# Two-layer decoder trunk: the up projections computed with x loaded and W moving, and transposed back through DVE squares and SBUF transfers

## The reference

```python
def causal_dwconv(x, w, b):      # width 3 here: each channel's own three taps over the sequence, plus a bias
    ...
def conv_ffn(h, w_up, conv_w, conv_b, w_down):
    u = causal_dwconv(h @ w_up, conv_w, conv_b)
    gate, val = jnp.split(u, 2, axis=-1)
    return (jax.nn.gelu(gate) * val) @ w_down

# in the trunk, for each layer:
#   x = x + mixer(rmsnorm(x, norm_mix));  x = x + conv_ffn(rmsnorm(x, norm_ffn), ...)
```

## The kernel before, in words

| stage | ACT | DVE |
|---|---|---|
| 2 | copy of the cross term (L387), after the block's last chunk | sum of the halves into h (L1006), then h times 1/rms (L1008) |
| 3 | last tap and bias into buf, 4 instructions (L430) | |
| 4, 5 | | the other two taps, 4 instructions each (L1102, L1108) |
| 6 | gelu, gate block (L434) | product of the halves, value block (L1118) |
| 7 | rounding into act (L438) | the rest into act (L1123), value block |

## Time and profile before

### The profile page before, as it was taken

One profiled execution on the slowest core, in us unless ns is written; L12 is line 12 of the kernel. 1 busy time (PEld: TensorE's weight loads), 2 busy tenths in 40 slices (PEclk: granted clock), 3 DMA queues, 4 the chain that ended last, 5 costly groups with the idle time before them and its releaser, 6 DMA issues.

```text
span 2245.3 us, 33233 instructions
## 1 busy us (share of the span) xinstructions
PE 2237.8 (100%) x12182; PEld 1930.9 (86%) x12182; DVE 1488.7 (66%) x1789; ACT 1158.0 (52%) x1452; POOL 7.7 (0%) x17
## 2 busy tenths in 40 slices
PE   9999999999999999999999999999999999999999
PEld 8888888888888888888888888888888888888887
DVE  7886766777677767545565556566777777674443
ACT  6654355555555555443455555555555555553333
POOL 0000000000000000000000000000000000000000
PEclk9999999999999999999999999999999999999999
DMA  7555655666666666556665454555656666666664
GB/s 271 185 175 165 193 173 187 185 190 188 187 188 191 190 186 189 189 185 196 194 219 177 158 189 161 167 185 172 196 178 195 182 191 187 187 190 212 203 202 140
DMA packets 216099, 420.93 MB, mean 187 GB/s; under 512 B 13029, under 2 KB 13045, under 8 KB 215888
## 3 DMA queue, kind: packets, MB, share of 16 engines
q1 hardware_dynamic: 214128, 413.59, 59.1%
q0 software_dynamic: 1456, 5.65, 0.7%
q10 hardware_dynamic: 432, 0.56, 0.1%
HBM read 417.62 MB, written 2.12 MB: 187 GB/s over the span
## 4 chain that ended last, share of the span: by engine, by line
PE 99%; DMA 0%; DVE 0%; ACT 0%; ACTq 0%; issue 0%
PE ps L685 48%; PE ps L689 24%; PE ps L738 5%; PE ps L739 5%; PE ps L740 5%; PE ps L711 4%; PE ps L713 4%; PE ps L712 4%; PE ps L777 0%; DMA x_res<-x_t 0%; PE ps L821 0%; PE ps L832 0%; PE ps L759 0%; PE ps L778 0%; PE ps L840 0%; PE ps L771 0%
## 5 line engine op out<-in xcount | busy, mean ns | idle before, releaser
L990 DVE TENSOR_TENSOR w_lo<-raw,w_hi 128x1024 fp32r<-128x1024 f32 x783 | 948.6, 1223 | 558.5 <-ACT w_hi L376 539.9
L376 ACT ACTIVATE w_hi<-raw 128x1024 fp32r<-128x1024 f32 x783 | 811.1, 1054 | 567.0 <-PE ps L689 358.1
L685 PE MATMUL ps<-xs,w_hi 128*128 128x512 f32 x3456 | 1086.7, 396 | 3.3 <-DVE w_lo L1419 2.7
L689 PEld LDWEIGHTS ps<-xs,w_lo 128*128 128x128 f32 x3456 | 649.2, 188 | 153.4
L689 PE MATMUL ps<-xs,w_lo 128*128 128x256 f32 x3456 | 679.1, 278 | 0.0
L685 PEld LDWEIGHTS ps<-xs,w_hi 128*128 128x128 f32 x3456 | 526.2, 189 | 4.5 <-DVE xs L1039 2.9
L685 PE MATMUL ps<-act,w_hi 128*128 128x512 f32 (+1 forms) x1216 | 382.3, 396 | 0.0
L689 PEld LDWEIGHTS ps<-act,w_lo 128*128 128x128 f32 x1216 | 228.4, 188 | 54.0
L689 PE MATMUL ps<-act,w_lo 128*128 128x256 f32 (+1 forms) x1216 | 239.0, 278 | 0.0
L685 PEld LDWEIGHTS ps<-act,w_hi 128*128 128x128 f32 x1216 | 185.2, 189 | 0.1
L738 PE MATMUL ps<-w_hi,xs 128*128 128x512 f32 x448 | 176.0, 393 | 0.0
(11 more groups left out here) (191 smaller groups left out, 1125.5 us busy)
## 6 DMA issues: line engine op xcount, KB each, us to landing
raw<-w_up SPq DMA_DIRECT2D x352, 512.0 KB, 3.7
raw<-w_in SPq DMA_DIRECT2D x191, 512.0 KB, 4.0
raw<-w_down SPq DMA_DIRECT2D x176, 512.0 KB, 4.7
raw<-w_out SPq DMA_DIRECT2D x64, 512.0 KB, 4.7
bias<-bias_line POOLq DMA_DIRECT2D x1, 2048.0 KB, 11.6
x_res<-x_t SPq DMA_DIRECT2D x3, 512.0 KB, 7.2
out_t<-x_res POOLq DMA_DIRECT2D x3, 512.0 KB, 5.8
gates_w<-w_gates POOLq DMA_DIRECT2D x1, 1024.0 KB, 5.3
```

Source lines behind the costliest of these rows:

```text
L376: act_f(w_hi[:, s, :, :], raw[:, s, :, :], ACT.Copy).then_inc(hi_ready, 1)
L685: return mm(ps[:, 4 * group + m, :], w_hi[:, s, u, m * P:(m + 1) * P], rhs, start=first and u == 0, stop=False)
L689: return mm(ps[:, 4 * group + m, 0:S], w_lo[:, s, u, m * P:(m + 1) * P], rhs[:, 0:S], start=False, stop=last and u == CT - 1)
L990: tt(w_lo[:, s, :, :], raw[:, s, :, :], w_hi[:, s, :, :].bitcast(F32), ALU.subtract).then_inc(lo_ready, 1)
```

## The change

The up projections of both layers take `chunk_values` in place of `chunk_products`. Their result comes out with the sequence on partitions, in two banks (4*half and 4*half + 1). The convolution needs channels on partitions, so it is turned in two steps:

1. DVE transposes the 32 x 32 squares of the two banks into `flip` (the place of `cross`): two instructions of 128 x 512. The ACT copy of the cross term and the DVE sum into h are gone.
2. SP issues sixteen transfers of 32 partitions x 1 KB, in four groups `move(n, i)`, i = 0 to 3, that bring each band of squares to its partitions in h. Group 0 is issued after the load of chunk 6 of the next block and waits for the transposes, group 1 after the load of chunk 7, groups 2 and 3 after the loads of chunks 0 and 1 of the block after that.

The sequence lies in h in another order, four segments of 64; the order of xs for the up projections is changed to fit (`x_seq`, `xs_seq`), for which DVE's `split_x` takes eight instructions of 128 columns instead of four of 256. The convolution's buffers have two more columns, zeroed once a layer, so that taps can be written shifted.

The stages move: the scaling by 1/rms to stage 7 (it waits for all sixteen transfers), the ACT tap to 8, the DVE taps to 9 and 10, gelu and product to 11, the rounding to 12 and the rest to 13. Stage 8 + c of a block runs in chunk c of the second block after it, ahead of stage c of the block before. The down projection's first block has its 22 chunks written out, with the last stages and moves among them.

```diff
-        self.cross_down = self.cross_up + 2 * PAIRS
+        self.cross_down = self.cross_up
...
+    flip = cross[:, :, :].rearrange("p b s -> p (b s)")
+    flip_by_seq = flip.rearrange("p (g k t r) -> p t g k r", g=QUADS, t=2, r=SQ)
+    flip_from = ps[:, :, :].rearrange("p b (k g c) -> p b g k c", g=QUADS, c=SQ)
+    flip_quads = flip.rearrange("p (g n) -> p g n", g=QUADS)
+    h_quads = h[:, :, :].rearrange("p b s -> p (b s)").rearrange("p (i n) -> p i n", i=QUADS)
+    h_tiles = h_quads.rearrange("p i (k n) -> p i k n", k=BT)
...
+        def move(n, i):
+
+            if i == 0:
+                sp.wait_ge(acc_drained, n + 1)
+            for g in range(QUADS):
+                sp.dma_start(h_quads[g * SQ:(g + 1) * SQ, i, :], flip_quads[i * SQ:(i + 1) * SQ, g, :]).then_inc(moved, 16)
...
-            with sp.Fori(0, PAIRS) as j:
+            for half in range(2):
+                for c in range(KC):
+                    load(w_up[l], ph.q_up + 2 * half, c, slice(half * D_FF, half * D_FF + NB), c)
+                    if half and c >= 6:
+                        move(ph.n_up, c - 6)
+            with sp.Fori(1, PAIRS) as j:
                 for half in range(2):
                     for c in range(KC):
                         load(w_up[l], ph.q_up + 4 * j + 2 * half, c, bass.ds(j * NB + half * D_FF, NB), c)
+                        if c < 2:
+                            move(ph.n_up + 2 * j + half - 2, 2 + c)
+                        if c >= 6:
+                            move(ph.n_up + 2 * j + half - 1, c - 6)
...
                 for c in range(KC):
                     split(ph.q_up + 4 * j, c)
+                    mlp_post(KC + c, ph, 0, j - 1)
                     mlp_post(c, ph, 1, j - 1)
                 for c in range(KC):
                     split(ph.q_up + 4 * j + 2, c)
+                    mlp_post(KC + c, ph, 1, j - 1)
                     mlp_post(c, ph, 0, j)
...
-                        chunk_products(ph.q_up + 4 * j + 2 * half, c, xs, CT * c, half, c == 0, c == KC - 1)
+                        chunk_values(ph.q_up + 4 * j + 2 * half, c, 4 * half, c == 0, c == KC - 1)
...
-            if stage == 2:
-                copy_cross(n, chunk_end(ph.q_up + 4 * j + 2 * half, KC - 1), half)
-            if stage == 3:
+            if stage == 8:
                 eng.wait_ge(normed, ph.normed_up + 2 * j + half + 1)
                 for t in range(BT):
...
-                    ins = act_f(buf[:, t, :], h[:, t, :], ACT.Identity, scale=w, bias=b)
+                    ins = act_f(by_quad(pad[:, t, 0:S]), h_tiles[:, :, t, :], ACT.Identity, scale=w, bias=b)
...
             if stage == 2:
-                drain_normed(n, ph.cross_up + 2 * j + half + 1, ph.normed_up + 2 * j + half + 1, half, h[:, :, :])
-            if stage == 4:
+
+                eng.wait_ge(chunk_used, chunk_end(ph.q_up + 4 * j + 2 * half, KC - 1))
+                step(v.transpose(flip_by_seq[:, 0], flip_from[:, 4 * half]))
+                v.transpose(flip_by_seq[:, 1], flip_from[:, 4 * half + 1]).then_inc(acc_drained, 1)
+                eng.wait_ge(acc_drained, n + 1)
+            if stage == 7:
+                eng.wait_ge(moved, 16 * QUADS * QUADS * (k + 1))
+                r = by_quad(rstd[:, 0:S])
+                scale = bass.AP(r.tensor, r.offset, [r.ap[0], r.ap[1], [0, BT], r.ap[2]])
+                tt(h_tiles, h_tiles, scale, ALU.mult).then_inc(normed, 1)
+                eng.wait_ge(normed, ph.normed_up + 2 * j + half + 1)
+            if stage == 9:
 
                 eng.wait_ge(tap_first, k + 1)
...
-                    ins = stt(out=buf[:, t, 2:S], in0=h[:, t, 0:S - 2], scalar=conv_at(ph.layer, 0, half, j, t),
-                              in1=buf[:, t, 2:S], op0=ALU.mult, op1=ALU.add)
+                    to = by_quad(pad[:, t, 2:S + 2])
+                    ins = stt(out=to, in0=h_tiles[:, :, t, :], scalar=conv_at(ph.layer, 0, half, j, t),
+                              in1=to, op0=ALU.mult, op1=ALU.add)
```

More of the change, by code:

```diff
@@ L38 @@
 PAIRS = D_FF // NB
+SQ = 32
+QUADS = P // SQ
 OUTB = D // NB
@@ L225, in build @@
     dve_step, act_step = sem("dve_step"), sem("act_step")
+    moved = sem("moved")
     tap_first, conv_done, gelu_done = sem("tap_first"), sem("conv_done"), sem("gelu_done")
@@ L310, in _ @@
                         load(w_up[l], ph.q_up + 4 * j + 2 * half, c, bass.ds(j * NB + half * D_FF, NB), c)
+                        if c < 2:
+                            move(ph.n_up + 2 * j + half - 2, 2 + c)
+                        if c >= 6:
+                            move(ph.n_up + 2 * j + half - 1, c - 6)
             for b in range(OUTB):
                 cols = slice(b * NB, (b + 1) * NB)
-                for c in DOWN_HEAD:
+                for c in range(FC) if b == 0 else DOWN_HEAD:
                     load(w_down[l], ph.q_down, FC * b + c, cols, c)
+                    if b == 0 and c in (0, 1, 8, 9):
+                        move(ph.n_down - 2 + c // 8, 2 + c % 8)
+                    if b == 0 and c in (6, 7):
+                        move(ph.n_down - 1, c - 6)
+                if b == 0:
+                    continue
                 with sp.Fori(*DOWN_TURNS) as t:
@@ L391, in split_x @@
             for t in range(j * BT, (j + 1) * BT):
-                ins = act_f(xs[:, t, 0, :], x_res[:, t, :], ACT.Copy, scale=param("gain", norm * KT + t))
+                to, x = xs[:, t, 0, :], x_res[:, t, :]
+                if norm % 2:
+                    to, x = xs_seq(to), x_seq(x)
+                ins = act_f(to, x, ACT.Copy, scale=param("gain", norm * KT + t))
             ins.then_inc(xs_hi, 1)
@@ L429, in mlp_post @@
                     b = conv_b_at(ph.layer, half, j, t)
[L430 removed]
+                    ins = act_f(by_quad(pad[:, t, 0:S]), h_tiles[:, :, t, :], ACT.Identity, scale=w, bias=b)
                 ins.then_inc(tap_first, 1)
[L432 removed]
+            if stage == 11 and half == 0:
                 eng.wait_ge(conv_done, k + 1)
[L434 to L435 removed]
+                act_f(pad_g[:, :, 0:S], pad_g[:, :, 0:S], ACT.Gelu_apprx_tanh).then_inc(gelu_done, 1)
+            if stage == 12 and half == 1:
                 g = ph.layer * PAIRS + j
                 eng.wait_ge(prod_ready, g + 1)
[L438 removed]
+                act_f(act[:, bass.ds(j * BT, BT), 0, :], pad_v[:, :, 0:S], ACT.Copy).then_inc(act_hi, 1)
         def conv_at(layer, tap, half, j, t):
@@ L650, in _ @@
                     split(ph.q_up + 4 * j + 2, c)
+                    mlp_post(KC + c, ph, 1, j - 1)
                     mlp_post(c, ph, 0, j)
             for b in range(OUTB):
-                for c in DOWN_HEAD:
+                for c in range(FC) if b == 0 else DOWN_HEAD:
                     split(ph.q_down, FC * b + c)
                     if b == 0:
+                        mlp_post(KC + c, ph, 0, PAIRS - 1)
                         mlp_post(c, ph, 1, PAIRS - 1)
@@ L1030, in split_x @@
             for t in range(j * BT, (j + 1) * BT):
-                ins = stt(out=xs[:, t, 1, :], in0=x_res[:, t, :], scalar=param("gain", norm * KT + t),
-                          in1=xs[:, t, 0, :].bitcast(F32), op0=ALU.mult, op1=ALU.subtract)
+                operands = [(xs[:, t, 1, :], x_res[:, t, :], xs[:, t, 0, :].bitcast(F32))]
+                if norm % 2:
+                    to, x, x_hi = operands[0]
+                    operands = [(xs_seq(to)[:, k], x_seq(x)[:, k], xs_seq(x_hi)[:, k]) for k in range(2)]
+                for to, x, x_hi in operands:
+                    ins = stt(out=to, in0=x, scalar=param("gain", norm * KT + t), in1=x_hi, op0=ALU.mult, op1=ALU.subtract)
             ins.then_inc(xs_lo, 1)
@@ L1453, in _ @@
                     stats_newton(2 * l + 1)
+                if c == 3:
+                    step.sync()
+                    for pad in (pad_g, pad_v):
+                        v.memset(pad[:, :, S:], 0.0).then_inc(pads_set, 1)
+                    eng.wait_ge(pads_set, 2 * (l + 1))
                 mlp_post(c, ph, 0, 0)
-            entered, per_pair = step.n, 2 * (2 * BT - 1)
+            entered, per_pair = step.n, 2 * 2 * BT
             with eng.Fori(1, PAIRS) as j:
```

47 lines of the change are left out of this document (31 added, 16 removed).

## The result

The changed kernel takes 2371.51 us (median of 4 runs, 2370.57 to 2375.28) against 2247.25 us before on the same chip: ratio 1.0556, interval 1.0538 to 1.0574. It is slower by 124 us. The forecast was 2226 us, and the range up to 2268 does not hold the result.

The account below looks back on a forecast made before the run. PE's own stream was taken as the bound: 2247.05 us less 23.1 for the matmul form plus 1.5 for waiting gave 2225.5, and the median 0.6 above the profiled execution gave 2226 us. Range 2222 to 2268; forecast's own 2223 to 2229.

Parts of the forecast that it names:

- rival 1: Up phase: the serial work through flip and h doesn't fit in PE's block; example loss 53 us, 2278 us; chance 0.25.
- the price of an issue: SP's queue: back to back, one issue starts each 0.41 to 0.52 us; 0.41 taken for small ones, sixteen a block.
- the third load: SP's queue, among the moves: issue 15, starting 5.75 us after the transposes and landing at 9.45, last four moves behind it.
- E: End of a block's transposes, from which the moves are timed; forecast steady 3.2 us after the end of its block.
- M: Time from the end of the transposes to the start of the scaling; the forecast had all moved after 9.9 us.
- the ring: Serial work from one block's transposes to the next's, through single-buffered flip and h: 21.6 us against a block's 21.76.
- d: Excess of the ring over PE's block, in us; claimed loss is 2 layers x (21 d - 3.7).
- PE's stream: Up projections: matmuls with W moving take 2.720 us a chunk against 2.786, saving 23.1 us over 352 chunks.
- Transposes: Added on DVE: two of 128 x 512 from PSUM a block, 0.74 us each, 1.41 us together.
- Margin: Each layer: E can drift from 3.2 to 6.9 us before PE starves, 3.7 us of cover.
- Rival 3: DMA engines: each small transfer costs a fixed time, bound above 0.50 us; at 0.8 us each, 2437 us; chance 0.04.
- Rival 4: Up projections: matmuls in the new form are not faster here, 0 saved, 2248 us; chance 0.01.

Follow-up runs that it names:

- half the count: Changed kernel with eight transfers of 64 partitions x 1 KB a block instead of sixteen of 32, output wrong: 2274.13 us, ratio 1.0119.
- eight and eight: Changed kernel with eight of each block's transfers issued by SP and eight by GpSimd, whole computation: 2224.89 us, ratio 0.9902.

## Why the prediction was wrong

The mechanism was right and named as rival 1, at 0.25. What failed is the size of one term, the price of an issue: "Back to back it starts an issue each 0.41 to 0.52 us; I take 0.41 for small ones". By it the third load was to start at 5.75 us and "All moved at E + 9.9"; in the medians of the trace that load starts at 9.1 us and the last move lands at 13.8.

- **The issue of a move.** A move read from SBUF starts 0.63 us after the one before it (590 ns and a gap). The rows behind the 0.41 were loads from HBM, and with HBM as source the moves take 421 ns and start 0.46 us apart, inside the 0.41 to 0.52 of those rows. From the transposes to the end of the last issue it is 12.0 us, not 7.8, and M is 13.8, not 9.9. The rest of the ring was right: 11.45 us in every run where the ring binds, forecast 11.7. So the ring is 25.3 us, not 21.6. In the prediction's own formula, d = 25.3 - 21.76 = 3.5: loss 2 x (21 x 3.5 - 3.7) = 140 us, 2224 + 140 = 2364 us, measured 2371.5.
- **The bounds.** I had 0.52 us as the slower end of an issue and did not carry it into the range: in the prediction's own path the third load is 14 issues behind, 14 x 0.11 = 1.5 us more of ring, d = 1.4 and 2275 us. The range stopped at d = 1.25, below even rival 1's own example of 2278 us. A forecast that fits by 0.2 us of 21.8, out of several estimated terms, was not worth 0.5.
- **PE's stream.** 23.1 us forecast, 23.5 found without moves, and a block of 21.71 us for 21.76. Right, and in part by luck: 44 blocks that are 0.58 us shorter than the 22.29 of before make 25.5 us, and 2 us of it went elsewhere, which was not looked into.
- **Transposes.** 0.72 and 0.67 us, 1.31 together (717.20 to 718.51); forecast 0.74 each and 1.41 together. Right to 0.1 us. The second starts 0.64 us after the first, for 512 elements, where the two plain passes of the earlier trace rows start 0.67 us apart: a transpose costs no more than a plain pass. The Trainium skill ("Vector Engine (DVE) Microarchitecture Reference", section 3.8) has one element per cycle per lane for it. The trace fits that in so far as it shows the pace of a plain pass, 1.25 ns an element with the fixed part in it; no run here shows the length of a cycle.
- **Margin.** PE's first wait in the up phase ends at 440.4 us, behind the second block's transposes, about as a margin of 3.7 us and d = 3.5 have it. The loss is paid in two places, not only at chunk 3 as forecast; the sum is the same, since d is paid once a block.
- **Landing behind the loads.** The prediction had M end by the queue: the last moves behind the third load. With the slow issues that path and SP's own end close together. The third load lands 13.0 us after the transposes and the first move behind it at 12.9; the last move lands at 13.8, 2.4 us after its issue, against 1.8 for the first moves of a block, which have no load ahead of them. The queue is worth some 0.5 us here. It is worth more with half the count and with HBM as source: M 11.6 and 12.5, above what the issues make.
- **Rival 3**, a fixed time of the engines for each transfer: the share of SP's queue is 60.7% of 2370.5 us against 59.1% of 2245.3, which is 112 us of all 16 engines for 704 moves, 0.16 us each; against the run without moves (60.5% of 2223.6) it is 94 us, 0.13 each. That is far under the 0.50 us at which the engines would be the bound, so rival 3 is out. The estimate of 0.8 us, from figures of the Trainium skill ("DMA: Bandwidth & Descriptors", section Bandwidth) that were measured from HBM, is not met by these moves. That page's statement that SBUF to SBUF transfers do not suffer from small descriptors ("Why small descriptors are slow (HBM only)") fits the run with 256 bytes a row: its share is 58.5% of 2362.8 us, 37 us over the run without moves, 0.05 us a move, so rows of a quarter of the bytes took 0.4 of the time.
- **Rival 4**, no gain from the form: refuted by the run without moves.
- **Not forecast:** the 40 table loads on ACT, 51 us. They cost nothing, as the run without them shows.

## What to carry to other kernels

When a buffer is single, add up the ring through it, from its filling to its next filling, and compare it with the time that a block has: below it everything is hidden, above it each block pays the excess, whatever the share of any engine. Count the issues of the queue inside the ring, and take their price from issues of the same kind of source. Where the sum comes near the block, a forecast should be as wide as the terms are uncertain. What helped here was another queue for half of the issues. Fewer bytes gave 7 us while sixteen issues set the time, and 40 us once there were eight; all sixteen issues on the other queue gave 61 of 147 us, and in that run the loads bunched. Breaking the ring with a second buffer for `flip` and h was not tried.

## What the hardware showed that was not expected

- The issue on SP depends on where the data comes from: 32 partitions of 1 KB from SBUF 590 ns, from HBM 421 ns; a weight load of 256 rows of 2 KB 372 ns. Neither rows nor bytes change it: with 64 partitions the second of a pair takes 590 to 596 ns, and with 256 bytes a row the median is 590 ns. The first of a group is shorter, 507 to 513 ns in the changed kernel.
- GpSimd issues such a move in 496 ns and starts one each 0.49 us, SP each 0.63 us.
- In the run with eight and eight, moves issued before SP's next load land in 1.7 to 2.1 us on either queue, and the ones issued after it in 3.1 to 4.0, on either queue. In the changed kernel the first move behind a load lands about when the load does, 6.5 us after the transposes, where the load is issued at 2.7 us and takes 3.8 in the median of the whole run. With a quarter of the bytes it is 6.4 us.
- One gelu ahead of the loop took away 40 table loads of 1.28 us inside it, 48 us of ACT on balance.
